# First weights of two stages fetched by the stage before them, and another order in the first group of a recurrence

## The reference

```
glu = proj[..., COL_GLU:COL_GATE]; u = glu_a * sigmoid(glu_b); u = dwconv(u); u = silu(layernorm(u))
xs, bm, cm, dt_f, dt_b = ssd_inputs(proj)           # conv + silu; softplus of the steps
# ssd_scan, for each direction:
cum   = cumsum(dt * a)                              # in chunks of 128 tokens
decay = exp(where(lower, cum_i - cum_j, -inf))      # "segments", one 128 x 128 per chunk and head
y_diag = (C B^T * decay) (x * dt)
states = B^T (exp(cum_end - cum) * dt * x);  h = h * exp(cum_end) + states
y_off  = exp(cum) * C h_in
y = y_f + flip(y_b) + ssm_d * xs
y = rmsnorm(y * silu(z)) ;  u_ssd = y @ w_ssm_out   # z = h @ w_in[:, COL_Z:COL_GLU]
mixed = (g_conv * u_conv + g_ssd * u_ssd) @ w_o     # g = sigmoid(h @ w_in[:, COL_GATE:])
```

## Time and profile before

| | us |
|---|---|
| median of 3 runs | 3691.31 |
| profiled execution, its own time | 3690.47 |
| its span on the core | 3688.8 |
| TensorE busy | 3561.5 (97%) |
| VectorE busy | 2059.8 (56%) |
| ScalarE busy | 1516.6 (41%) |

### The profile page before, as it was taken

The page is one execution under the profiler, slowest core; times in us unless marked ns, Lnnn a source line. Parts: engine busy times, 40 slices in busy tenths (PEclk is TensorE's granted clock), DMA queues, the critical chain, the costliest instruction groups (busy, mean ns, idle before and its releaser), DMA issues. The chain is left out here.

```text
span 3688.8 us, 49207 instructions
## 1 busy us (share of the span) xinstructions
PE 3561.5 (97%) x20281; PEld 2926.9 (79%) x20281; DVE 2059.8 (56%) x2837; ACT 1516.6 (41%) x2423; POOL 358.4 (10%) x331
## 2 busy tenths in 40 slices
PE   8999899899899999999989999999999999999999
PEld 6888688788788888887668778888988887876887
DVE  6987677665534453446676563444354644456743
ACT  5664578543323332222543342233352323255322
POOL 3671000000000000002121000000000000153000
PEclk9999899999999999999999999999999999999999
DMA  6345544333233333333320233333222333411332
GB/s 204 98 126 181 176 124 146 100 96 92 81 98 96 97 94 97 98 92 100 83 67 3 78 94 97 97 96 99 86 86 80 92 97 92 142 48 46 92 97 86
DMA packets 597303, 364.79 MB, mean 99 GB/s; under 512 B 16823, under 2 KB 578824, under 8 KB 596568
## 3 DMA queue, kind: packets, MB, share of 16 engines
q1 hardware_dynamic: 592487, 349.91, 32.1%
q10 hardware_dynamic: 4592, 11.73, 0.9%
HBM read 345.70 MB, written 15.89 MB: 98 GB/s over the span
## 5 line engine op out<-in xcount | busy, mean ns | idle before, releaser
L1219 PE MATMUL later_bank<-arena 128*128 128x512 f32 (+1 forms) x6792 | 1439.1, 373 | 19.2 <-DVE arena L1191 15.2
L1219 PEld LDWEIGHTS later_bank<-arena 128*128 128x128 f32 x6792 | 1195.9, 189 | 256.7 <-DVE arena L1191 24.5
L1183 ACT ACTIVATE arena<-arena 128x1024 fp32r<-128x1024 f32 (+2 forms) x550 | 570.7, 1038 | 1563.4 <-PE later_bank L1219 766.7
L1219 PE MATMUL middle_bank<-arena 128*128 128x512 f32 x4944 | 1141.9, 392 | 24.8 <-DVE arena L1191 16.8
L1219 PEld LDWEIGHTS middle_bank<-arena 128*128 128x128 f32 x4944 | 928.4, 188 | 239.7 <-DVE arena L1191 25.5
L1191 DVE TENSOR_TENSOR arena<-arena 128x1024 fp32r<-128x1024 f32 (+2 forms) x550 | 668.0, 1215 | 586.9 <-ACT arena L1183 584.5
L1219 PE MATMUL front_bank<-arena 128*128 128x512 f32 (+3 forms) x1776 | 350.8, 357 | 7.5 <-DVE arena L1191 4.2
L1219 PEld LDWEIGHTS front_bank<-arena 128*128 128x128 f32 (+1 forms) x1776 | 292.0, 189 | 58.2 <-DVE arena L1191 4.7
L1410 POOL TENSOR_TENSOR arena<-arena 128x512 f32<-128x512 f32 x120 | 168.2, 1402 | 119.0 <-ACT arena L1708 103.3
L1219 PE MATMUL ssd_bank<-arena 128*128 128x512 f32 x576 | 146.0, 405 | 4.4 <-DVE arena L1191 4.4
L1865 DVE SCALAR_TENSOR_TENSOR arena<-front_bank,columns,arena 128x510 f32<-128x510 f32 (+1 forms) x224 | 126.7, 627 | 21.1 <-ACT arena L1636 19.2
(11 more groups left out here) (467 smaller groups left out, 3060.7 us busy)
## 6 DMA issues: line engine op xcount, KB each, us to landing
arena<-in_w_in SPq DMA_DIRECT2D x114, 512.0 KB, 3.8
arena<-in_ffn_w_gate SPq DMA_DIRECT2D x76, 512.0 KB, 3.7
arena<-in_ffn_w_up SPq DMA_DIRECT2D x76, 512.0 KB, 3.7
arena<-in_w_mlp SPq DMA_DIRECT2D x64, 512.0 KB, 3.8
arena<-in_w_ada SPq DMA_DIRECT2D x48, 512.0 KB, 5.9
arena<-in_ffn_w_down SPq DMA_DIRECT2D x48, 512.0 KB, 3.9
arena<-scratch_cum SPq DMA_DIRECT2D x64, 256.0 KB, 6.3
arena<-in_gm_w_in SPq DMA_DIRECT2D x32, 512.0 KB, 3.8
```

The costliest lines, as they stand in the source:

```text
L1183: act.activation(self.high[q % self.AHEAD][:, 0:kb * cols], self.raw[g % RING][:, 0:kb * cols], ACT.Copy).then_inc(self.high_done, 1)
L1219: ins = pe.matmul(out, still, moving, start=first and n_pass == 0, stop=last and n_pass == 2)
```

## The change

1. The weights' ring lies at one place in SBUF in the front, the recurrence and the middle (`arena.ring`), and a `Flow` may begin at another slot than 0 (`base`), where the stage before left off. The arrays of `dt` move out of its way.
2. `Flow.fetch`: as the last loads of its stage, SyncE fetches the first steps of the next stage: two for the recurrence, from the front, and three for the merge, from the recurrence. They have semaphores that no stage clears. `load` leaves them out.
3. In group 0, SyncE fetches two rows of `cum` first; ScalarE splits step 0 ahead of `keep_turned`, and makes two segments ahead of the last three turned pieces; TensorE makes the first z product between the turning of x and that of B and the context; VectorE splits step 1 and weighs the ends early, and makes `skip` only when the group's sum needs it.
4. In the other groups silu of z stands behind `keep_turned` and `split_high` of the next group, and `group_out` behind `split_low` of the second z.
5. TensorE makes products that nobody reads at the end of the front (6) and at the end of the recurrence (2), 512 columns each in full float32.
6. A new semaphore, `cb_masked`, keeps the last chunk state from being written into `cb_bank` before VectorE has masked it.

```diff
+    def slot(self, g):
+        return (g + self.base) % RING
+    def fetch(self, sp, sems, sources):
+        for n, (sem, src) in enumerate(zip(sems, sources)):
+            g = len(self.steps) + n
+            sp.wait_ge(self.products, self.unit_after[g - RING + 1])
+            k, cols = src.shape[0] // P, src.shape[1]
+            sp.dma_start(self.raw[self.slot(g)][:, 0:k * cols].rearrange("p (k n) -> p k n", k=k), src.rearrange("(k p) n -> p k n", p=P)).then_inc(sem, 16)
...
     def load(...):
+                if g < len(self.fetched):
+                    continue
...
 # Front.sync
         flow.load(sp, [j for kind, n, j in self.units[last:]])
+        flow.fetch(sp, self.core.first_weights["ssd"], [w_in[:, COL_Z + b * P:COL_Z + (b + 1) * P] for b in range(2)])
 # Front.tensor, last
+        for n in range(self.IDLE_PRODUCTS):
+            pe.matmul(self.ada_banks[0][:, :], core.ident[:], core.resid[:, 0, :], start=True, stop=True)
...
 # ssd_stage, sync
+            for k in range(2):
+                load_row(0, k)
             load_b_and_context(0)
             load_c(0)
-            flow.load(sp, jobs[0:2])
-            for k in range(2 * R):
+            for k in range(2, 2 * R):
                 load_row(0, k)
-            flow.load(sp, jobs[2:RING])
+            flow.load(sp, jobs[0:RING])
...
+            flow.fetch(sp, core.first_weights["middle"], [w_in[:, COL_GATE + b * P:COL_GATE + (b + 1) * P] for b in range(3)])
 # tensor
                 turned_tokens(g)
+                if g == 0:
+                    flow.multiply(pe, z_jobs[0][0])
                 turned_rest(g)
...
-                flow.multiply(pe, z_jobs[g][0])
+                if g:
+                    flow.multiply(pe, z_jobs[g][0])
...
+                    if j == CH - 2:
+                        pe.wait_ge(cb_masked, g + 1)
...
+            for n in range(2):
+                pe.matmul(cb_bank[:, :], core.ident[:], core.resid[:, 0, :], start=True, stop=True)
 # scalar
+            def silu_z(g):
+                flow.wait_emptied(act, z_jobs[g][1], 0)
+                act.activation(z, z, ACT.Silu).then_inc(z_silu, 1)
             for g in range(G):
-                keep_turned(g)
                 if g:
+                    keep_turned(g)
                     flow.split_high(act, 3 * g + 1)
+                    silu_z(g - 1)
                     gate(g - 1)
                     first_z(g)
                     outer_states(g)
                 else:
                     flow.split_high(act, 0)
+                    keep_turned(0, 0, 2)
                     flow.split_high(act, 1)
-                    for k in range(2 * R):
+                    for k in range(2):
+                        segment(0, k)
+                    keep_turned(0, 2, 5)
+                    for k in range(2, 2 * R):
                         segment(0, k)
...
-                flow.wait_emptied(act, z_jobs[g][1], 0)
-                act.activation(z, z, ACT.Silu).then_inc(z_silu, 1)
+            silu_z(G - 1)
             gate(G - 1)
 # vector, in the loop over groups
+                if g == 0:
+                    flow.split_low(dve, 1)
+                    weigh_ends(0)
...
-                if g:
-                    group_out(g - 1)
...
-                flow.split_low(dve, 3 * g + 1)
...
+                if g:
+                    flow.split_low(dve, 3 * g + 1)
+                    group_out(g - 1)
+                    weigh_ends(g)
                 order.wait(cb_mark)
+                dve.sem_inc(cb_masked, 1)
...
                 flow.split_low(dve, 3 * g + 3)
+                if g == 0:
+                    make_skip()
```

More of the change, by code:

```diff
@@ L122, in allocate_core @@
     core.nc, core.ins = nc, ins
+    core.first_weights = {name: [nc.alloc_semaphore(f"{name}_first_weights{n}") for n in range(count)] for name, count in (("ssd", 2), ("middle", 3))}
     sb = lambda name, shape: ctx.enter_context(nc.sbuf_tensor(name, shape, F32))
@@ L164, in allocate_core @@
     arena = core.arena = Arena(nc, "arena", ARENA)
+    arena.ring = [arena.f(RING_AT + STEP_COLS // T * n, STEP_COLS // T) for n in range(RING)]
     core.xs, core.ssm_gate = arena.f(XS_AT, XB), arena.f(SSM_GATE_AT, DB)
@@ L542, in _, with make_skip @@
             flow.split_low(dve, 0)
-            dve.wait_ge(skip_in, 16)
-            for half in range(2):
-                rows = slice(64 * half, 64 * half + 64)
-                order.then(dve.tensor_copy(skip[rows, :], d_all[rows, half::2]))
+            def make_skip():
+                dve.wait_ge(skip_in, 16)
+                for half in range(2):
+                    rows = slice(64 * half, 64 * half + 64)
+                    order.then(dve.tensor_copy(skip[rows, :], d_all[rows, half::2]))
             def group_out(g):
@@ L603, in ssd_stage @@
     st.close()
+    return flow.slot(len(flow.steps))
 def first_block(core, scratch):
@@ L609, in first_block @@
     dt, dta, masks = flat(0), flat(1), Recurrence(core)
-    front_blocks(core, ins["x"][0], ins["ctx"][0], scratch, dt, dta, masks)
-    ssd_stage(core, masks, scratch["cum"], scratch["bc"], scratch["context"])
+    last = front_blocks(core, ins["x"][0], ins["ctx"][0], scratch, dt, dta, masks)
+    return ssd_stage(core, masks, scratch["cum"], scratch["bc"], scratch["context"], last.slot(len(last.steps)))
 F2 = 2816
@@ L1123, with __init__ @@
     AHEAD = 2
-    def __init__(self, st, arena, first, banks, jobs):
+    def __init__(self, st, arena, first, banks, jobs, base=0, fetched=()):
         per = STEP_COLS // T
+        assert first == RING_AT
+        self.base, self.fetched, landings, self.landing = base, fetched, [0] * RING, []
         flat = lambda ap: ap.rearrange("p b t -> p (b t)")
-        self.raw = [flat(arena.f(first + per * n, per)) for n in range(RING)]
+        self.raw = [flat(piece) for piece in arena.ring]
         self.low = [flat(arena.r(first + per * n, per)) for n in range(RING)]
@@ L1135, in __init__ @@
         count, done, served, held = 0, {"act": 0, "dve": 0}, 0, [None] * len(banks)
+        for g in range(sum(j.steps for j in jobs)):
+            if g < len(fetched):
+                self.landing.append((fetched[g], 16))
+            else:
+                landings[self.slot(g)] += 16
+                self.landing.append((self.landed[self.slot(g)], landings[self.slot(g)]))
         self.unit_after, self.split_steps, self.splits_before = [0], [], []
@@ L1922, in front_blocks @@
     front.st.close()
+    return front.flow
 class NormBefore:
@@ L3419, in middle_blocks @@
     mix = Mix(rg, gates_dram)
[L3420 removed]
+    flow = Flow(rg.st, rg.arena, RING_AT, rg.flow_banks, [j for stage in (merge, mlp, swiglu, mix) for j in stage.jobs], base, core.first_weights["middle"])
     weight, made = rg.few(DB), rg.st.sem("both_weights")
```

50 lines of the change are left out of this document (27 added, 23 removed).

## The result

| | before | changed |
|---|---|---|
| median, us (5 runs each) | 3691.31 (3688.94 to 3697.62) | 3673.48 (3672.17 to 3675.98) |
| ratio | | 0.9949, 95% interval 0.9938 to 0.996 |
| span of the profiled execution | 3688.8 | 3671.8 |

The change takes 17.8 us off the median and 17.0 off the profiled span. The forecast was 3676.3, with a range of 3670.5 to 3683.

The account below looks back on a forecast made before the run. TensorE is busy 97% of the span, so only its idle time and its lower clock could pay. Border 3.5, front 0, groups 2 to 7 4.2 and group 0 6.5 make 14.2 off 3690.47: 3676.3 us, range 3670.5 to 3683.

Parts of the forecast that it names:

- Border, 3.5: Border from recurrence to middle: weights have landed, so ScalarE splits at once; 3.8 us less 0.3 for two unread products.
- Its clock, taken as 0 of 0 to 3.0: Middle's first product: a held clock would give another 3.0 us; no gain taken, since it fell after 4.03 us idle.
- Front, 0: End of the front: two added loads and six unread products just fit, costing 0; ends 0 and -1.7 us.
- Groups 2 to 7, 4.2: Later recurrence groups: silu and group_out leave the path, so the 0.7 us wait per group goes six times, 4.2 us.
- The rival of ScalarE's loop: Later groups: ScalarE's loop, some 32.2 us, overruns 33.1 if rows land late; only 10 us won, 3680.5; chance 0.14.
- Group 0, 6.5: First recurrence group: diagonal part 10.3 us earlier, less 0.7 lost later, less 3.1 for the clock: 6.5 us.
- six segments and the first z, 11.0 + 1.65: Group 0 on ScalarE: after the last turned pieces at 433.8, these take 11.0 + 1.65 us, to 446.4.
- 9.6 without a fall: Group 0: upper end of its gain, 9.6 us, if TensorE's clock does not fall.
- the rival whose clock holds: Unread products carry the clock over both borders: group 0 gives 9.6, border 6.5, 20.3 us in all, 3670.2; chance 0.12.
- the gain in group 0 is hidden: Group 0: late cum rows or segments waiting for w_in leave 2 us; sum under 7.4, 3684 to 3690; chance 0.09.
- The rest, 0: The ring's place, its first slot, the unchanged number of splits and cb_masked move no work: 0 us.
- the 1.9 of my estimate from the Trainium skill's counts: Each cold start: 8 matmuls more or fewer at 0.24 us make 1.9 us either way; sum between 12 and 16.

Follow-up runs that it names:

- r_changed: The changed kernel run and profiled once more, with no edit: median 3673.69 us, ratio 0.9953 to the kernel before.
- e2: The changed kernel with silu of z ahead of the next group's turned pieces and group_out ahead of the masks again: median 3680.88 us, ratio 0.9959.
- e4: The kernel before with one edit, skip made behind the last low split of group 0: median 3688.27 us, ratio 0.9984.

## Why the prediction was right, step by step

The forecast was 14.2 us off the execution's time, and 17.0 off the span were found. By its terms:

- *Border, 3.5:* 8.65 to 5.03, 3.6. The path was as drawn: one high split, one low split, the two unread products costing 0.3. *Its clock, taken as 0 of 0 to 3.0:* the middle's first six us had PEclk 0.76 for 0.50, which is 1.6 us. The clock did fall, but for a shorter time.
- *Front, 0:* 6.59 us from TensorE's last small product to the recurrence, for 6.60. Right. The recurrence starts at 424.29, past the 424 that I named as a sign against me; but the 0.7 us lie ahead of the unread products, and r_changed starts at 422.71.
- *Groups 2 to 7, 4.2:* 235.6 to 231.5, 4.1; seven starts 33.1 apart. Right in size and cause. The five groups that I read as 33.8 each are one of 33.1 (group 2) and four of 33.8 to 34.1. The rival of ScalarE's loop did not happen: in group 6 ScalarE ends its segments at 663.83, 32.3 us after the group's start for my 32.9, and waits for the next turning. The 32.2 that the rival has for the loop is not worked out there. What the step left out is what e2 and e4 showed: the old order would have cost 1.6 to 2 us more after a fast group 0, so the move is worth 6.1 in the changed kernel.
- *Group 0, 6.5:* 48.6 to 41.8, 6.8, and 7.0 in the second execution. The size is right, and in r_changed so is the working: the first z product in 8.61 us, 2.0 us of idle time, 3.71 for the diagonal part, which ScalarE's segments bound. In the first execution another thing took the same room, and that its 6.8 lies so near 6.5 is luck. The step that went wrong there is "six segments and the first z, 11.0 + 1.65": the gate's split in it has no wait for weights, though SyncE puts their load behind eight rows. It cost 2.09 us. The clock then fell in the diagonal part, 5.29 us for 3.72. The loss also sets a bound that I did not see: with two steps fetched, the six executions with the new order and the fetch took 41.4 to 41.8 us whether the first z product ran in 5.74 or in 8.61 us. My end "9.6 without a fall", and the 20.3 of the rival whose clock holds, could not be had without the third step, which gave 38.7 us, some 10 less than before. My rival "the gain in group 0 is hidden" named the wait for weights and priced it at 4.5. Its sum is wrong as it stands: 2 in place of 6.5 leaves 9.7 in all, or 8.0 with the front's 1.7, so 3681 to 3682.5 and not 3684 to 3690.
- *The rest, 0:* 0.7 us more stand ahead of the recurrence, and some 1.5 less behind the middle's first six us. Of the latter the traces show a likely cause, the clock. From the middle's first product to the end of the span the thirteen profiled executions took 2968.3 to 2976.0 us. In stretches of 5 us, TensorE's busy time times the part of the clock that it was not granted makes 23.0 to 29.2 us there (27.8 in the kernel before, 23.0 in the changed one); taken off, it leaves 2944.2 to 2947.0. No run tested it.

The sum 6.8 + 4.1 + 3.6 + 1.6 - 0.7 + 1.5 is 16.9 of the 17.0; its last term is what was left over, so it proves nothing by itself. The forecast of 14.2 was too low by the border's clock (1.6) and by the last two terms (0.8 together), and only by 0.3 in group 0.

The signs named for being right came: VectorE no longer waits for `ssm_d` at the start, the first z product starts 2.35 us behind the barrier, the diagonal part at 449.61, the groups are 33.1 us, the gap at the border is 3.31 us. The last came in part: the clock behind the border was low for some three us, not for six.

One product took 5.76 and 8.61 us in two executions of the same code. The Trainium skill (TensorE: Matmul & The Clock Gate, the part on the HAM clock gate) says that the clock's monitor does not start with the kernel; the two times fit that, and no run here shows the monitor itself. The swing here, 2.9 us, is more than the 1.9 of my estimate from the Trainium skill's counts. That estimate also called its 0.24 us a matmul the difference between rows 3 and 6; these products differ by 2.83 us in 24 matmuls, 0.12 each, because the clock of rows 3 was low for 6.1 of the 8.56 us only.

## What to carry to other kernels

Before adding work to the front of a stage, ask what that stage's first wait would be if its weights were there already: fetching them from the stage before was worth 9 us in the first group, and the new order without it made that group 2.3 us longer than before. A small constant that stands last in a DMA queue and first in an engine's is the cheapest of all to move; here VectorE, and TensorE behind it, waited for 16 KB. And where a second engine is slower per group than the first (here ScalarE, by 0.7 us), a faster start takes away its lead and the long groups begin earlier (1.6 to 2 us in e4 and e2), so the two have to be changed together.

## What the runs showed of the hardware

- Around gaps of 1.3 to 3.3 us the granted clock differs between executions, of one and the same code too. With gaps of 1.33 to 1.70 us and of 1.29 us, and 1.06 us of turning between them, the next 24 matmuls took 5.74 to 5.76 us in four executions, 7.10 in one, 8.61 and 8.62 in two; the longest first gap, 1.70 us, stood ahead of one of the fast four. Behind 3.31 us the clock fell in five of six. Behind gaps of 0.96 and 0.39 us it did not fall in the two executions that had them.
- A product that nobody reads, 128 x 512 in full float32, takes 0.9 us (5.40 us for six); ahead of a barrier at which TensorE stood idle for 6.6 us, six of them left the start of the next stage where it was.
- Profiled executions of the changed kernel had the recurrence start at 424.29 and 422.71, and other low stretches in later stages; and the stretch from the middle to the end took 2968.3 to 2976.0 us over all kernels, though none of them changes it behind its first products. So a difference of a few us between two spans says nothing, while the length of the groups or of the border says it to a tenth.
